# Four wide matmuls without a use are put among the output products of each S5 block

## The chip, the cores and the metric

The kernel runs on one core of a Trainium2 chip. The metric is the device time of one execution in microseconds (us). The engines are called as in the profile: PE is TensorE, with its weight loads shown apart as PEld; DVE is VectorE, ACT is ScalarE, POOL is GpSimd and SP is SyncE. The names with a q (DVEq, SPq, ACTq) are the engines' own sequencers and DMA queues.

## The reference

It is a trunk of two layers over a sequence of 512 tokens of width 1024. Each layer is a half-step SwiGLU feed-forward (FFN), a token mixer, and a second half-step FFN, each behind an RMSNorm with a shift, a scale and a gate from a conditioning vector. The mixer of layer 0 is retention. The mixer of layer 1, which the change touches, is an S5 state space layer:

```python
    bu = jnp.einsum('blgk,gpk->blgp', ug, B_bar)
    a = jnp.broadcast_to(A_bar, (1, L, G, P))
    _, states = lax.associative_scan(combine, (a, bu), axis=1)   # s[t] = A_bar * s[t-1] + bu[t]
    y = jnp.einsum('gkp,blgp->blgk', C_mat, states).real.reshape(Bsz, L, Dm)
    y = jax.nn.gelu(y + d_skip.astype(f32) * uf).astype(u.dtype)
    y1, y2 = jnp.split(y @ w_glu, 2, axis=-1)
    return y1 * jax.nn.sigmoid(y2)
```

There are 64 groups of 16 channels with 64 complex states each.

## The kernel before

All activations are held transposed, with 128 channels on the partitions and the 512 tokens along the free axis, as 8 such tiles. Every large product is made in three parts from a high and a low half of each operand (`mm3`, lines 1309 to 1311). These are single-pass fp32r matmuls with 128x128 weights and 512 moving columns; this text calls them wide. The weights come in chunks of 1024 rows by 256 columns into two buffers, are copied to `w_hi` by ACT and subtracted to `w_lo` by DVE. Chunk n is complete when the semaphore `w_lo_done` stands at n + 2. Chunk 134 (`C_GLU`) is the first one of the S5 layer's GLU and lies in `w_hi[0]`, `w_lo[0]`.

The S5 mixer works on 8 blocks (b) of 8 groups (g). The sequence is cut into 64 pieces of 8 tokens, so that a group's piece is one column of 128 numbers, and a block has 8 x 64 = 512 columns. For each block:

- PE makes the piece inputs of the scan (`states(b)`, line 1505): one plain fp32 matmul for each group, 64 moving columns wide, into bank b % 2 of PSUM. This text calls 64-column fp32 matmuls narrow. The trace shows each of them as two instructions with a weight load each.
- DVE turns them, scans them along the pieces and turns them back into `sc_buf` and `ss_buf` (`scan(b)`), and then signals `sc_done`.
- PE makes the outputs (`outputs(b)`, lines 1518, 1520 and 1521): for each group three narrow matmuls into bank 4 or 6, and then signals `y_done`.
- ACT applies the gelu, writes the block to DRAM and reads it back in token order; ACT and DVE split it into `h_hi` and `h_lo` for the GLU product (`a5_lo` counts them).

PE's order is written out by hand: `states(0)`, and then for each b `states(b + 1)` and `outputs(b)`. The GLU chunks follow behind the last output. SP loads the tables of blocks 6 and 7 behind `y_done` of blocks 2 and 3 in its counting (it waits for counts 3 and 4); they take the place of tables that are used up by then.

Of the kernel before, what the change touches and what calls it, by code (L numbers as in the profile page):

```python
# [13 lines left out]
P = 128  # L14
# [22 lines left out]
C_GLU = 134  # L37
# [53 lines left out]
def build(nc, ins, out):  # L91
    x_d, c_d, pos_d = ins["x"], ins["c"], ins["positions"]
    ctx = ExitStack()
    with ctx:
        def sem(name):
            return ctx.enter_context(nc.semaphore(name))
# [6 lines left out]
        def sb(name, shape, dt=F32, at=None):  # L103
            size = 4 * int(np.prod(shape[1:]))
            if at is None:
                at = place["end"]
                place["end"] = (at + size + 31) // 32 * 32
                assert place["end"] <= nc.sbuf_usable_end, (name, place["end"])
            return nc.alloc_sbuf_tensor_at(name, shape, dt, offset=at)
# [8 lines left out]
        w_hi = [sb(f"w_hi{s}", [P, 8, CW], F32R) for s in range(2)]  # L118
# [82 lines left out]
        ps = ctx.enter_context(nc.psum_tensor("ps", [P, 8, L], F32))  # L201

        w_landed = [sem(f"w_landed{s}") for s in range(2)]
        w_hi_done, w_lo_done, w_used = sem("w_hi_done"), sem("w_lo_done"), sem("w_used")
# [1101 lines left out]
        def _(pe):  # L1306
# [6 lines left out]
            def chunk(n, k, xh, xl, r0, r, bank, first, last, ready=None):  # L1313

                pe.wait_ge(w_lo_done, n + 2)
                s = k % 2
                for t in range(r):
                    if ready is not None:
                        pe.wait_ge(ready[0], ready[1] + t + 1)
                    for c in range(2):  # L1320
                        m = mm3(ps[:, bank + c], w_hi[s][:, t, c * P:(c + 1) * P], w_lo[s][:, t, c * P:(c + 1) * P],
                                xh[:, r0 + t], xl[:, r0 + t], first and t == 0, last and t == r - 1)
                m.then_inc(w_used, 1)
# [173 lines left out]
            def s5():  # L1497
                def states(b):
                    pe.wait_ge(us_in[b], 16)
                    pe.wait_ge(tb_in[b], 16)  # L1500
                    if b >= 2:
                        pe.wait_ge(v_read, b - 1)
                    for g in range(GB):
                        cs = slice(g * NC, (g + 1) * NC)
                        m = nc.tensor.matmul(ps[:, b % 2, cs], tables[b][:, R_WIN + g * P:R_WIN + (g + 1) * P],  # L1505
                                             us[:, b, cs], start=True, stop=True)
                    m.then_inc(v_done, 1)

                def outputs(b):
                    s = b % 2  # L1510
                    pe.wait_ge(sc_done, b + 1)
                    if b >= 2:
                        pe.wait_ge(gelu_done, b - 1)
                    for g in range(GB):
                        cs = slice(g * NC, (g + 1) * NC)
                        o = ps[:, 4 + 2 * s, cs]
                        yw = tables[b][:, R_YS + g * P:R_YS + (g + 1) * P]
                        nc.tensor.matmul(o, tables[b][:, R_MT + g * P:R_MT + (g + 1) * P], us[:, b, cs],  # L1518
                                         start=True, stop=False)
                        nc.tensor.matmul(o, yw, sc_buf[s][:, cs], start=False, stop=False)  # L1520
                        m = nc.tensor.matmul(o, yw, ss_buf[s][:, cs], start=False, stop=True)  # L1521
                    m.then_inc(y_done, 1)

                states(0)
                for b in range(KT):
                    if b + 1 < KT:
                        states(b + 1)
                    outputs(b)
                pe.wait_ge(v_read, KT)
                for dp in range(OUT_PAIRS):  # L1530
                    n = dp * 2 + C_GLU
                    pe.wait_ge(x_done, dp + (5 * OUT_PAIRS + 1))
                    chunk(n, 0, h_hi, h_lo, 0, 8, 0, True, True, ready=None if dp else (a5_lo, 0))
                    chunk(n + 1, 1, h_hi, h_lo, 0, 8, 2, True, True)
# [18 lines left out]
            for q in range(ADA_FIRST):  # L1553
# [3 lines left out]
                for c in range(4):  # L1557
                    m = nc.tensor.matmul(ps[:, 6, c:c + 1], ada_acc[:, c * P:(c + 1) * P], ones[:, 0:1],
                                         start=True, stop=True)
# [10 lines left out]
            ffn(2)  # L1570
            norm(4)
            s5()
            norm(5)
            ffn(3)
# [78 lines left out]
```

## Time and profile before

| what | value |
|---|---|
| median of 3 runs | 2487.16 us (2482.06 to 2487.32) |
| the profiled execution, its own time | 2487.07 us |
| its span, first to last instruction | 2485.3 us |
| mean granted clock of PE over the span | 0.927 |
| PE busy | 2242.6 us, 90% |
| DVE busy | 1167.7 us, 47% |
| ACT busy | 631.3 us, 25% |
| POOL busy | 37.5 us, 2% |

Positions below are microseconds from the start of the span. The granted clock (PEclk) has two levels in this trace: 1.00 is 2.4 GHz and 0.50 is 1.2 GHz. A matmul's duration is longer than the distance to the next one, because they are pipelined. What one costs in a run of them is the distance from start to start, which is read from the timeline or from a stretch and its count.

### The profile page before, as it was taken

The page shows a single profiled execution, that of the slowest core. Times are in us where ns is not written, and L with a number is a line of the kernel's source. Part 1 is how long each engine was busy: PE and PEld are TensorE (multiplying, and loading weights), DVE is VectorE, ACT ScalarE, POOL GpSimd, SP SyncE. Part 2 cuts the span into 40 slices and gives each one's busy share as a digit, 9 for nine tenths or more (in the row PEclk, how much of TensorE's full clock was granted, in tenths as well). Part 3 has the DMA queues.
Part 4 walks back from the last instruction along what each step waited for, and adds up shares of the span by engine and source line. Part 5 has one row for each costly group of instructions (what it writes and reads, how often), then busy time and mean ns, then how long its engine had stood idle before and what let it go on. Part 6 is the DMA issues. An engine that isn't in the chain of part 4 may idle for free.

```text
span 2485.3 us, 26565 instructions
## 1 busy us (share of the span) xinstructions
PE 2242.6 (90%) x10363; PEld 1862.4 (75%) x10363; DVE 1167.7 (47%) x1443; ACT 631.3 (25%) x531; POOL 37.5 (2%) x45
## 2 busy tenths in 40 slices
PE   2499999889999898999998999999949988999996
PEld 1488888778888786888876767678839866888884
DVE  4755544455455325555476655434444334333331
ACT  2222222232223213222221322221220124344221
POOL 1000000000000000000000000000000000000000
PEclk9899999889999998999999889899965698999997
DMA  6245634432232233555454344434683122322220
GB/s 223 68 154 183 203 122 154 163 110 89 68 105 89 84 102 102 173 173 194 130 179 150 129 120 124 117 107 132 219 274 103 50 68 68 101 90 96 93 93 34
DMA packets 264433, 313.07 MB, mean 126 GB/s; under 512 B 31568, under 2 KB 218280, under 8 KB 263096
## 3 DMA queue, kind: packets, MB, share of 16 engines
q1 hardware_dynamic: 224664, 282.66, 34.6%
q10 hardware_dynamic: 39712, 29.63, 4.1%
q8 instruction: 38, 0.62, 0.1%
q14 instruction: 19, 0.16, 0.0%
HBM read 288.93 MB, written 27.53 MB: 127 GB/s over the span
## 4 chain that ended last, share of the span: by engine, by line
PE 50%; issue 34%; DVE 8%; ACT 4%; DMA 2%; ACTq 2%; POOL 1%; SPq 0%; DVEq 0%; POOLq 0%
PE ps L1309 14%; PE ps L1311 14%; PE ps L1310 14%; ACT w_hi L470 1%; DVE ada_acc L756 1%; PE ps L1518 1%; PE ps L1520 1%; PE ps L1521 1%; PE ps L1415 1%; ACTq L607 1%; DVE w_lo L745 1%; PE ps L1505 1%; DVE ys L897 1%; DVE tabs L897 1%; ACT h_hi L470 1%
## 5 line engine op out<-in xcount | busy, mean ns | idle before, releaser
L1309 PE MATMUL ps<-h_hi,w_lo 128*128 128x512 f32 x1792 | 719.7, 402 | 54.5 <-DVE w_lo L745 28.0
L1310 PE MATMUL ps<-h_lo,w_hi 128*128 128x512 f32 x1792 | 711.7, 397 | 0.0
L1311 PE MATMUL ps<-h_hi,w_hi 128*128 128x512 f32 x1792 | 711.3, 397 | 0.0
L745 DVE TENSOR_TENSOR w_lo<-w_raw,w_hi 128x2048 fp32r<-128x2048 f32 (+1 forms) x175 | 392.6, 2243 | 513.6 <-ACT w_hi L470 513.4
L470 ACT ACTIVATE w_hi<-w_raw 128x2048 fp32r<-128x2048 f32 (+1 forms) x176 | 328.9, 1869 | 478.7 <-PE ps L1311 170.0
L1309 PEld LDWEIGHTS ps<-h_hi,w_lo 128*128 128x128 f32 x1792 | 346.5, 193 | 130.0 <-DVE w_lo L745 28.6
L1311 PEld LDWEIGHTS ps<-h_hi,w_hi 128*128 128x128 f32 x1792 | 344.9, 192 | 74.3
L1310 PEld LDWEIGHTS ps<-h_lo,w_hi 128*128 128x128 f32 x1792 | 346.0, 193 | 70.8
L1309 PE MATMUL ps<-g_hi,w_lo 128*128 128x512 f32 x832 | 331.1, 398 | 10.8 <-DVE g_lo L1158 6.9
L1310 PE MATMUL ps<-g_lo,w_hi 128*128 128x512 f32 x832 | 329.9, 396 | 0.0
L1311 PE MATMUL ps<-g_hi,w_hi 128*128 128x512 f32 x832 | 329.8, 396 | 0.0
L756 DVE SCALAR_TENSOR_TENSOR ada_acc<-ada_raw,csil,ada_acc 128x512 f32<-128x512 f32 x224 | 168.5, 752 | 138.2 <-DMA ada_raw<-in_ada_w 126.4
L1309 PEld LDWEIGHTS ps<-g_hi,w_lo 128*128 128x128 f32 x832 | 156.8, 189 | 49.6 <-issue 7.2
L1311 PEld LDWEIGHTS ps<-g_hi,w_hi 128*128 128x128 f32 x832 | 156.7, 188 | 38.5
L1310 PEld LDWEIGHTS ps<-g_lo,w_hi 128*128 128x128 f32 x832 | 156.8, 189 | 37.9
L470 ACT ACTIVATE g_hi<-s_buf 128x1024 f32 (+1 forms) x48 | 51.0, 1062 | 373.0 <-DVE s_buf L873 343.5
L873 DVE TENSOR_TENSOR s_buf<-s_buf,ps 128x1024 f32<-128x1024 f32 x44 | 53.7, 1221 | 156.9 <-PE ps L1311 156.7
L563 ACT ACTIVATE s_buf<-ps 128x1024 f32<-128x1024 f32 x44 | 45.2, 1028 | 211.2 <-PE ps L1311 211.1
L1309 PE MATMUL ps<-w_hi,h_lo 128*128 128x256 f32 x256 | 74.0, 289 | 7.0 <-DVE w_lo L745 7.0
L877 DVE TENSOR_TENSOR g_lo<-s_buf,g_hi 128x1024 f32 (+1 forms) x44 | 53.9, 1225 | 54.5 <-ACT g_hi L470 54.5
L532 ACT ACTIVATE sq<-x_sb 128x1024 f32<-128x1024 f32 (+1 forms) x24 | 25.4, 1059 | 205.1 <-DVE x_sb L825 159.1
L1310 PE MATMUL ps<-w_lo,h_hi 128*128 128x256 f32 x256 | 73.6, 288 | 0.0
(205 smaller groups left out, 1710.0 us busy)
## 6 DMA issues: line engine op xcount, KB each, us to landing
w_raw<-in_ffn_w_in SPq DMA_DIRECT2D x88, 1024.0 KB, 6.7
ada_raw<-in_ada_w SPq DMA_DIRECT2D x128, 512.0 KB, 5.4
w_raw<-in_ffn_w_out SPq DMA_DIRECT2D x32, 1024.0 KB, 7.3
w_raw<-in_ret_w_in SPq DMA_DIRECT2D x24, 1024.0 KB, 5.2
w_raw<-in_ffn_w_out SPq DMA_DIRECT2D x16, 768.0 KB, 4.5
tb<-s_rec SPq DMA_DIRECT2D x6, 2048.0 KB, 10.3
ada_first<-in_ada_w SPq DMA_DIRECT2D x8, 1024.0 KB, 14.3
w_raw<-in_ret_w_out SPq DMA_DIRECT2D x8, 1024.0 KB, 5.0
```

Of the source, the lines that this page charges most:

```text
L470: copy = lambda o, i: nc.scalar.activation(o, i, ACT.Copy)
L532: nc.scalar.activation(sq[:], x_sb[:, tiles, :], ACT.Square).then_inc(sq_done, 1)
L563: nc.scalar.activation(s_buf[:], ps[:, 0:2], ACT.Silu).then_inc(silu_done, 1)
L607: act.dma_start(to[:, :, j * SK:P], lag_out[:, :, 0:P - j * SK]).then_inc(lag_stored, 16)
L745: V.tensor_tensor(w_lo[k % 2][:, 0:r, :], w_raw[k % 2][:, 0:r, :], raw_f32(w_hi[k % 2][:, 0:r, :]), ALU.subtract).then_inc(w_lo_done, 1)
L756: st(V.scalar_tensor_tensor(out=into, in0=raw[:, t], scalar=c, in1=into, op0=ALU.mult, op1=ALU.add))
L873: V.tensor_tensor(s_buf[:], s_buf[:], ps[:, 2:4], ALU.mult).then_inc(prod_done, 1)
L877: V.tensor_tensor(g_lo[:, bass.ds(i * 2, 2), :], s_buf[:], raw_f32(g_hi[:, bass.ds(i * 2, 2), :]), ALU.subtract).then_inc(g_lo_done, 1)
L897: tt = lambda o, a, b, op: st(V.tensor_tensor(o, a, b, op))
L1309: nc.tensor.matmul(o, wl, xh, start=start, stop=False)
L1310: nc.tensor.matmul(o, wh, xl, start=False, stop=False)
L1311: return nc.tensor.matmul(o, wh, xh, start=False, stop=stop)
```

## The change

Behind the three output products of every second group (g = 0, 2, 4, 6), PE issues one more matmul: 128x128 weights from `w_hi[0]`, 512 moving columns from `w_hi[0]` as well, into bank 7, which nothing reads in this stage. That is 4 in each block and 32 in all. Since these read `w_hi[0]`, PE waits once, between `states(0)` and the loop over the blocks, until chunk 134 is complete.

```diff
@@ -1519,9 +1519,12 @@
                                          start=True, stop=False)
                         nc.tensor.matmul(o, yw, sc_buf[s][:, cs], start=False, stop=False)
                         m = nc.tensor.matmul(o, yw, ss_buf[s][:, cs], start=False, stop=True)
+                        if g % 2 == 0:
+                            nc.tensor.matmul(ps[:, 7], w_hi[0][:, 0, 0:P], w_hi[0][:, 0:2, :], start=True, stop=True)
                     m.then_inc(y_done, 1)
 
                 states(0)
+                pe.wait_ge(w_lo_done, C_GLU + 2)
                 for b in range(KT):
                     if b + 1 < KT:
                         states(b + 1)
```

## Rows read from the trace of the kernel before

**Rows 1.** The page: busy tenths and granted clock in 40 slices of 62 us.

```profile
PE   2499999889999898999998999999949988999996
PEclk9899999889999998999999889899965698999997
```

**Rows 2.** Stretch: busy (count) of PE, PEld, DVE, ACT, POOL; clock; DMA share, GB/s.

```profile
1859.24:1961.69 102.45, 102.35 (x480) 102.35 (x481) 46.31 (x62) 7.96 (x13) 7.36 (x7) 0.50 0.24 77
```

**Rows 3.** Timeline (start, us, what): chunk 134's low half, and the first states.

```profile
1808.72 2.29 DVE L745 TENSOR_TENSOR w_lo<-w_raw,w_hi 128x2048 fp32r<-128x2048 f32 x1 [3.40 <-ACT w_hi L470]
...
1841.04 7.09 PE L1505 MATMUL ps<-us,tb 128*128 128x64 f32 x32 [20.74 <-DMA us<-u_dram]
```

**Rows 4.** Waits from 1840 to 1990: us in total, times, longest.

```profile
PE ps L1518 <- DVEq L1230: 11.2, 1, 11.2
...
ACT h_hi L470 <- DMA sq<-y_dram: 4.4, 1, 4.4
```

**Rows 5.** The chain that ended last: the S5 stage's first output and the GLU's first product.

```profile
1859.34 0.69 PE ps L1518 x2
...
1962.00 0.53 PE ps L1309
```

**Rows 6.** Timeline where the narrow matmuls end and the GLU's wide ones begin.

```profile
1961.69 0.33 PEld L1309 LDWEIGHTS ps<-h_hi,w_lo 128*128 128x128 f32 x1
1961.76 0.77 PE L1309 MATMUL ps<-h_hi,w_lo 128*128 128x512 f32 x1
1961.90 0.33 PEld L1310 LDWEIGHTS ps<-h_lo,w_hi 128*128 128x128 f32 x1
...
1962.33 0.63 PE L1310 MATMUL ps<-h_lo,w_hi 128*128 128x512 f32 x1
```

**Rows 7.** Timeline: the first and the last of seven wide matmuls at clock 0.50.

```profile
731.41 0.63 PE L1311 MATMUL ps<-h_hi,w_hi 128*128 128x512 f32 x1
...
733.97 0.63 PE L1311 MATMUL ps<-h_hi,w_hi 128*128 128x512 f32 x1
```

**Rows 8.** Timeline in the third FFN: fp32 transposes between wide matmuls, clock 1.00.

```profile
1425.77 0.39 PE L1311 MATMUL ps<-h_hi,w_hi 128*128 128x512 f32 x1
1426.00 1.03 PE L1403 MATMUL ps<-ident,xs 128*128 128x128 f32 x8
...
1427.11 0.39 PE L1310 MATMUL ps<-h_lo,w_hi 128*128 128x512 f32 x1
```

**Rows 9.** Stretches around two rises of the clock: us, PE busy (x), PEclk, DMA.

```profile
1594.60:1598.00 3.40, 3.40 (x15) 0.50 0.95 307
1598.00:1601.40 3.40, 3.40 (x9) 0.50 0.00 1
1601.50:1604.90 3.40, 3.40 (x16) 1.00 0.00 0
...
1963.30:1966.70 3.40, 3.40 (x10) 0.50 0.27 92
1966.70:1970.10 3.40, 3.40 (x17) 1.00 0.28 63
```

**Rows 10.** Groups of PE's matmuls from 1594.6 to 1598.0 (L1417's left out).

```profile
L1415 PE MATMUL ps<-ys,xs 128*16 128x128 f32 x5 | 1.6, 411 | 0.0
L1309 PE MATMUL ps<-h_hi,w_lo 128*128 128x512 f32 x2 | 1.4, 712 | 0.0
...
L1310 PE MATMUL ps<-h_lo,w_hi 128*128 128x512 f32 x1 | 0.6, 628 | 0.0
L1311 PE MATMUL ps<-h_hi,w_hi 128*128 128x512 f32 x1 | 0.6, 628 | 0.0
```

**Rows 11.** DVE's timeline: first and last step of one S5 block's scan.

```profile
1887.01 1.41 DVE L897 TENSOR_TENSOR tur<-ps,tb 64x512 f32<-64x512 f32 x2 [1.13 <-PE ps L1505]
...
1892.69 0.68 DVE L897 TENSOR_TENSOR sc_buf<-scanned,tb 128x504 f32<-128x504 f32 x1
```

**Rows 12.** DMA issues of the page: KB each, median us to landing.

```profile
tb<-s_rec SPq DMA_DIRECT2D x6, 2048.0 KB, 10.3
```

## The prediction

> **What bounds the kernel now.** I began with the page's two lines in 40 slices [rows 1]. PE is busy nine tenths and more nearly everywhere, so the kernel's time is PE's time, at the clock that PE is granted. The dip of the clock row to 5 and 6 in slices 30 to 32 is the stage of the change: PE is busy 4 tenths in slice 30 and 9 tenths in 31 and 32, at half clock.
>
> Second, the stretch from the first output product to the first GLU product, 1859.24 to 1961.69 [rows 2]: 102.45 us, PE busy for 102.35 of them, clock 0.50 all through. DVE works 46.3 us of it, ACT 8.0, POOL 7.4, and the DMA share is 0.24. It holds 480 narrow instructions: 8 blocks of 48 outputs, and 6 blocks of 16 states (those of blocks 0 and 1 ran ahead, 32 instructions at 1841.04 [rows 3]). 102.4 / 480 = 0.2133 us each.
>
> Third, the waits [rows 4]. PE's last one before the GLU is for DVE's first scan, 11.2 us, and ends at 1859.3; behind it PE waits for nobody. The chain of waits says the same [rows 5]: it leaves DVE at 1859.3 and then stays on PE, narrow matmul after narrow matmul, and goes over to the GLU's wide ones at 1962.0 without a wait between. What is put among the output products is therefore on the path that sets the end, whole, if it takes PE's time.
>
> **The change, part by part.**
>
> *The wait.* It asks for chunk 134's low half. DVE made that at 1808.72, done at 1811.0 [rows 3]. PE comes to the new wait behind the first 16 instructions of 1841.04, some 30 us later. It costs one sequencer step on an engine that afterwards stands idle for 11.2 us waiting for the scan [rows 4]: 0. Behind it stand `states(1)` and all outputs; had the semaphore been late, those would be too, but it has 30 us in hand.
>
> *The 32 wide matmuls.* None is removed, none moved, no DMA is added. All 32 come behind 1859.34. They write bank 7, which no other engine uses here, and read a buffer that is next overwritten after the first GLU chunk. So there is only PE's time to price, and the trace has no such matmul between narrow ones at this clock. I take it from three neighbouring rows.
>
> - At half clock a wide one follows a wide one after (733.97 - 731.41) / 6 = 0.427 us [rows 7].
> - The step from narrow to wide [rows 6]: weight loads start at 1961.69 (wide) and 1961.90, and the second wide matmul at 1962.33. The first wide one's weights took one slot of 0.213, as a narrow one's do, and it then streamed for 0.427. Put between two narrow ones it adds one slot of weights and its streaming time, and hides one narrow load behind its streaming: net 0.427.
> - At full clock both changes of kind are seen [rows 8]. From the wide one at 1425.77 to the first of 8 transposes 0.23 us pass, the plain pace of wide ones. From there to the second wide matmul behind them (1427.11) it is 1.11 us; 8 transposes at 0.110, which is their 1.03 us less the last one's own 0.27 over 7, and one wide one at 0.23 give 1.11. So changing kind costs nothing to speak of.
>
> Sum: 32 x 0.427 = 13.7 us, all on the path, if the clock stays at 0.50.
>
> Bounds. The low one: the engine could run further ahead with weight loads than I read, so that each filler also hides its own load: 0.427 - 0.213 = 0.213, 6.8 us in all. The high one: the recorded starts at the change of kind, 1961.76 against 1962.33, are 0.57 apart, and the chain gives that one 0.53 us [rows 5]; at about 0.54 each it would be 17.3 us. I take 0.427, since it is what the slots on both sides of the change add up to.
>
> *The clock.* This is the term that could be larger than the sum: narrow instructions need about half as long at full clock. In this trace the clock never rises during 102 us of unbroken narrow work [rows 2]. It does rise after the GLU begins: at 1963.30:1966.70 PE ran 10 matmuls, all wide, at 0.50, and the next stretch stands at 1.00 [rows 9]. What a mixture does is seen elsewhere. From 1594.6 to 1598.0, 4 wide ones (4 x 0.427 = 1.7 of 3.4 us) stand with 11 small fp32 ones [rows 9, 10], and the stretch behind it, 9 wide ones, is still at 0.50; only the one after that is at 1.00 [rows 9]. In the changed kernel a filler of 0.43 us stands behind every 12 narrow instructions (2.56 us), and a block's 16 states (3.4 us) have none: 4 x 0.427 = 1.7 us of 15.4 us in a block, 11% wide. That is far thinner than the mixture above, half of it wide, which did not raise it. I take it that the clock stays at 0.50.
>
> The Trainium skill, TensorE: Matmul & The Clock Gate (Part 1, What's actually happening), says that "the default state is throttled, and activity releases the throttle". Taken as meaning busy time, that rule would have S5 at full clock already, since PE has no gap there; the trace has 0.50 at 102.35 of 102.45 us busy, so it does not hold here in that form. Taken as meaning that more columns released it, it is the first rival below; on the forecast's sum it has no bearing.
>
> *What is late next.* Each block takes PE 64 x 0.2133 + 1.7 = 15.4 us in place of 13.65 (the last 13.65 less 3.4 for want of states). DVE's scan takes 6.4 us from 1887.01 to 1893.4 [rows 11] and still ends before its outputs start; the tables need 10.3 us from issue to landing [rows 12] and are asked for two blocks ahead of their use. ACT's last read-back, which it waits for 4.4 us [rows 4], starts with the last output and so moves along with the GLU. No new wait. Nothing behind the stage changes. One thing may shift by chance: how many wide matmuls the GLU runs at half clock before the rise, some 11 before [rows 9], at 0.427 - 0.23 = 0.2 us each: up to 2.2 us either way.
>
> Total: 2487.07 + 13.7 = 2500.7 us against the profiled execution, which lies 0.1 us below the median of the runs, 2487.16. I predict 2500.8.
>
> **The rivals.**
>
> *A. The fillers raise the clock (faster).* The place is the same stretch. At full clock the narrow ones would come every 0.110 us, as the transposes with the same weight load do [rows 8], and the fillers every 0.23: 480 x 0.110 + 32 x 0.23 = 60.2 us in place of 102.4. Blocks would take 64 x 0.110 + 4 x 0.23 = 8.0 us, still longer than the scan's 6.4, and two of them longer than a table's 10.3. The GLU would start at full clock: -2.2. With a first block at half clock (15.4 - 8.0): +7.4. That is 2487.1 - 42.2 - 2.2 + 7.4 = 2450.1. It decides from the point at which full clock holds for a quarter of the stretch: being at full clock all through saves 116.1 - 60.2 = 55.9 us, and 13.7 is a quarter of that (0.245). For it: something wide does raise the clock, always. Against it: the half-wide mixture, and the thin share of 11% [rows 9, 10].
>
> *B. Half of each filler is hidden* (the low bound, weights loaded ahead): 2487.1 + 6.8 = 2493.9. For it speaks that the second wide one's load starts 0.43 us ahead of it (1961.90, 1962.33) [rows 6]; against it the even 0.213 of narrow ones [rows 2].
>
> *C. Each filler costs its change of kind too* (the high bound): 2487.1 + 17.3 = 2504.4. Against it: the transposes among wide ones, which pay nothing for it [rows 8].
>
> *D. It makes no difference.* That needs a wait of PE in the stretch in which the fillers could lie. There is 0.1 us of idle time [rows 2]. It would give 2487.
>
> **How the numbers follow.** Forecast 0.83; A 0.06; B 0.05; C 0.04; D 0.02. The time is the forecast's. Its own spread is the chance shift at the GLU's start and that of the runs shown, 2482 to 2487: 2495 to 2504. The range is 2493 to 2506, which takes in B and C and leaves A and D outside, with under 2 in 10. A measurement of this kernel tells 0.2%, 5 us, from no change. Slower by more than that: forecast, C and nearly all of B, 0.91. Within it: D and a little of B, 0.03. Faster: A, 0.06.
>
> **What the changed profile would show.** The stretch from the first output product to the first GLU product should be 116.1 us long (right: 115 to 117), with 512 instructions of PE and the clock at 0.50 throughout. A filler's neighbours should stand 0.64 us apart (0.213 + 0.427) where they stood 0.213 apart. PE should wait for nothing behind 1859, and the new wait should show no idle time. Wrong in the direction of A: any stretch of S5 at 1.00, and narrow instructions 0.11 us apart. Wrong in B or C: the same clock, and a stretch of 109 or 120 us. The prediction fails if the chip counts narrow fp32 work for more towards the clock than the 102 us at 0.50 let me think, so that one filler in twelve tips it.

## The result, and the profile after

The changed kernel takes 2503.09 us (median of 12 runs, 2496.64 to 2507.17), the kernel before 2488.65 us (12 runs, 2480.27 to 2495.9). The ratio is 1.0053, 95% interval 1.0038 to 1.0068: slower by 13.2 us, with 9.5 to 16.9 for its interval. The prediction had 13.7, and 2500.8 us in a range of 2493 to 2506.

The profiled execution took 2499.44 us, its span is 2497.6. First the stretches of PE between the first output product and the first GLU product, and at the GLU's start, as in [rows 2, 9]. The first row has all engines, the others PE alone, in which PE busy (count), the granted clock and the DMA share follow the length.

```profile
1858.34:1974.44 116.10, 116.00 (x512) 112.93 (x512) 46.35 (x62) 7.96 (x13) 7.38 (x7) 0.50 0.21 68
1975.20:1978.60 3.40, 3.40 (x10) 0.50 0.22 80
1978.60:1982.00 3.40, 3.40 (x17) 1.00 0.33 75
```

The stretch was 102.45 us with 480 instructions and is 116.10 with 512: 13.65 us more, at clock 0.50 from end to end. DVE, ACT and POOL do what they did. The GLU runs at half clock at first, and the clock rises behind some 10 wide matmuls in a row, where it was some 11 before.

The chain of waits, which answers to [rows 5], and PE's waits from 1840 to 1990, to [rows 4]:

```profile
1858.43 0.69 PE ps L1518 x2
1859.12 0.43 PE ps L1520 x2
1859.55 0.43 PE ps L1521 x2
1859.98 0.53 PE ps L1523
...
1974.75 0.53 PE ps L1309
```

```profile
PE ps L1505 <- DMA us<-u_dram: 20.5, 1, 20.5
PE ps L1518 <- DVEq L1230: 11.0, 1, 11.0
```

Line 1523 is the added matmul. It stands on the chain, and PE still has only the two waits that lie ahead of the outputs. The timeline shows one of them with its neighbours; PEld are the weight loads, whose starts are the better clock:

```profile
1859.67 0.33 PEld L1523 LDWEIGHTS ps<-w_hi 128*128 128x128 f32 x1
1859.74 0.77 PE L1523 MATMUL ps<-w_hi 128*128 128x512 f32 x1
1859.88 0.76 PEld L1518 LDWEIGHTS ps<-us,tb 128*128 128x128 f32 x2
...
1860.52 0.55 PEld L1520 LDWEIGHTS ps<-sc_buf,tb 128*128 128x128 f32 x2
```

Between the load at 1859.88 and that at 1860.52 lie two narrow loads, 0.64 us in place of 2 x 0.213: the next load starts later by the 0.427 that the added one streams. That is the 0.213 + 0.427 that the prediction named. The new wait asks for a value that DVE's work of 1807.32 to 1809.61 gave, some 31 us before the first states at 1840.39.

### The profile page after: what moved, and what is told of

The parts are those of the page before. It is cut to its first block, busy times and chain, and to the rows that moved or that the text cites. A ratio compares the mean times of both kernels' runs of the same rounds, so it can differ in the third digit from the quotient of the medians.

```text
span 2497.6 us, 26629 instructions
## 1 busy us (share of the span) xinstructions
PE 2255.0 (90%) x10395; PEld 1871.1 (75%) x10395; DVE 1167.9 (47%) x1443; ACT 631.4 (25%) x531; POOL 37.5 (2%) x45
## 4 chain that ended last, share of the span: by engine, by line
PE 51%; issue 33%; DVE 7%; ACT 4%; ACTq 2%; DMA 1%; POOL 1%; DVEq 0%; SPq 0%; POOLq 0%
PE ps L1309 14%; PE ps L1310 14%; PE ps L1311 14%; ACT w_hi L470 1%; DVE ada_acc L756 1%; PE ps L1415 1%; PE ps L1521 1%; PE ps L1520 1%; ACTq L607 1%; PE ps L1518 1%; PE ps L1505 1%; DVE ys L897 1%; DVE w_lo L745 1%; PE ps L1523 1%; DVE tabs L897 1%
## 5 line engine op out<-in xcount | busy, mean ns | idle before, releaser
L1311 PEld LDWEIGHTS ps<-g_hi,w_hi 128*128 128x128 f32 x832 | 156.4, 188 | 38.4
```

The lines of the kernel that those rows point to most:

```text
L1311: return nc.tensor.matmul(o, wh, xh, start=False, stop=stop)
```

## Experiments

All use one helper and the added wait, unless a diff says otherwise:

```python
                def wide(cols=512):
                    nc.tensor.matmul(ps[:, 7, 0:cols], w_hi[0][:, 0, 0:P], w_hi[0][:, 0:2, :], start=True, stop=True)
```

Each was timed in turns with the kernel before on the same chip; e1 to e4, e5 to e8 with e12, and e9 to e11 ran on three different chips, so ratios compare them better than medians do. "The stretch" is the time from the first output's weight load to the first GLU product's, from the experiment's one profile.

### The price of one: e6, e5, e1

e6 keeps the wait and leaves out the matmuls.

```diff
                 states(0)
+                pe.wait_ge(w_lo_done, C_GLU + 2)
```

> Only the added wait on chunk 134, no added matmul. Theory T: 0 us, within 0.2% of before, the stretch 102.45 us. If the wait had a part in the loss, the start of the second block's states would be later than right behind the first's.

Ratio 0.9998 (0.9982 to 1.0013), and the stretch is as before:

```profile
1855.30:1957.65 102.35, 102.35 (x480) 102.35 (x480) 46.33 (x62) 7.97 (x13) 7.37 (x7) 0.50 0.24 77
```

The wait costs nothing that shows.

e5 has the change's 32 matmuls with 256 moving columns.

```diff
+                        if g % 2 == 0:
+                            wide(256)    # the moving columns are w_hi[0][:, 0, 0:256]
```

> The change with 256 moving columns in each added matmul in place of 512. Theory T says that what one adds is its place in the row of weight loads or its streaming time, whichever is longer: at half clock a load's slot is 0.213 us and 256 columns stream for 0.213 us, so each adds 0.213 us, 6.8 us in all; the stretch from the first output to the first GLU product is 109.3 us at clock 0.50 and the kernel 7 us above before. A rival in which a change between narrow fp32 and fp32r work has a fixed price of its own would show more than 0.213 us each: with 0.32 us, 112.7 us.

Ratio 1.0021 (1.0008 to 1.0034), 5.2 us. The profile is sharper:

```profile
1861.98:1971.16 109.18, 109.18 (x512) 109.18 (x512) 46.34 (x62) 7.96 (x13) 7.37 (x7) 0.50 0.23 73
```

(109.18 - 102.35) / 32 = 0.213 us each, half of what 512 columns cost. The change of kind has no price of its own.

e1 puts one behind every group, 64 in all.

```diff
+                        if True:
+                            wide()
                     m.then_inc(y_done, 1)
```

> The wide matmul stands behind every group (8 in a block, 64 in all) in place of every second. Theory T (each adds 0.427 us to PE's path at half clock and the clock stays down, since a burst of nothing but wide ones is what raises it): the stretch from the first output to the first GLU product is 102.45 + 64 x 0.427 = 129.8 us at clock 0.50, the kernel 27.3 us above before. Rival A (a denser sprinkling raises the clock): some stretch of S5 stands at 1.00 and narrow instructions come every 0.11 us there; the stretch is well under 100 us.

Ratio 1.0092 (1.0075 to 1.0108), 22.9 us by the ratio and 23.1 by the medians (2512.83 against 2489.68).

```profile
1862.10:1991.55 129.45, 129.45 (x544) 123.39 (x544) 46.36 (x62) 7.97 (x13) 7.38 (x7) 0.50 0.19 61
```

The stretch grew by 27.1 us, 0.423 each, as expected, and even twice the density leaves the clock at 0.50. The kernel lost some 4 us less than the stretch, which lies just outside the ratio's interval of 18.7 to 26.9 us. Behind the stage this profile has 521.0 us against 523.6 before, and one fall of the clock fewer in the GLU; yet the two profiled executions, 2514.42 and 2487.07 us, are 27.4 apart. No run takes that apart, and it stays open.

### The same matmuls where PE is idle: e2, e3, e4

If only an unbroken run of wide matmuls raises the clock, that run can be had for nothing: PE stands idle for 11 us ahead of the first outputs [rows 4]. e2 moves all 32 there.

```diff
                     if b + 1 < KT:
                         states(b + 1)
+                    if b == 0:
+                        for _ in range(32):
+                            wide()
                     outputs(b)
```

> The same 32 wide matmuls, but all in a row in PE's idle time between the second block's states and the first block's outputs, none among the outputs. Theory T: the first 11 us of them lie in the wait for DVE's scan and cost nothing; they raise the clock before the outputs begin, and the narrow ones then run every 0.11 us for as long as the clock holds. In the GLU it held 23.9 us after each rise; about 4 of those pass before the outputs, so some 20 us of S5 run at 1.00, which saves about 19 us: the stretch takes 83 us, the kernel about 2469 by the time of before 2488. Rival N (narrow fp32 work pulls the clock down at once, whatever came before): the clock falls back to 0.50 within some 4 us of the first output, stretch about 100 us, kernel within 3 us of before. Rival H (raised once, unbroken narrow work holds it): stretch 480 x 0.11 = 53 to 60 us, kernel 42 to 49 us below before.

Ratio 0.9949 (0.9921 to 0.9977), but its 12 runs are two groups: five at 2462 to 2466 and seven at 2483 to 2494. The profile is of the second group:

```profile
1852.10:1860.90 8.80, 8.80 (x34) 6.87 (x33) 6.28 (x6) 3.20 (x2) 0.00 (x0) 0.84 0.49 160
1860.90:1863.40 2.50, 0.31 (x3) 0.26 (x3) 2.18 (x4) 0.00 (x0) 0.23 (x1) 1.00 0.16 53
1863.40:1865.10 1.70, 1.70 (x18) 1.70 (x17) 1.64 (x3) 0.00 (x0) 0.82 (x1) 1.00 0.00 0
1865.10:1963.40 98.30, 98.30 (x464) 98.30 (x463) 44.54 (x60) 7.96 (x13) 6.31 (x6) 0.50 0.25 81
```

The burst raised the clock, PE then stood idle for 2.2 us, ran 18 narrow instructions at 1.00, and the clock fell. So there is a way to raise it; in this run the gain was gone after 2 us of outputs, and the stretch of some 100 us is that of rival N. The five runs at 2462 to 2466 gain what theory T expected and more, but none of them was profiled.

e3 is e2 with the change's 4 in each block, e4 e2 with 8 in each block.

```diff
+                        if g % 2 == 0:     # e4: if True
+                            wide()
```

> The burst of 32 in PE's idle time, and the change's 4 wide ones in each block as well. It asks if the change's spacing, which can't raise the clock, can hold it once it is up. Theory T by itself does not say; the traces have stretches this thin on both sides. If held throughout: 480 x 0.11 + 32 x 0.23 = 60 us, the kernel some 42 us below before. If it falls after the 23.9 us as without fillers: 83 us + about 11 us for the fillers left at half clock = 92 us, kernel 10 us below before. Rival N: 116 us as in the changed kernel.

> The burst, and 8 wide ones in each block. If this density holds the clock: 480 x 0.11 + 64 x 0.23 = 67.5 us for the stretch, kernel 35 us below before; blocks are then 8.9 us. If it doesn't: some 20 us at 1.00 and the rest at half clock, about 105 us, kernel 2 us above before. Rival N: 130 us, kernel 27 above.

e3: ratio 0.9983 (0.9954 to 1.0012), again two groups, six runs at 2465 to 2478 and six at 2493 to 2507. e4: 1.0094 (1.0079 to 1.0108), one group. The profile of e3 is of its better group:

```profile
1848.90:1858.70 9.80, 9.80 (x34) 7.68 (x33) 7.16 (x8) 3.19 (x2) 0.00 (x0) 0.73 0.49 158
1858.70:1860.20 1.50, 0.38 (x3) 0.20 (x2) 1.25 (x3) 0.00 (x0) 0.18 (x1) 1.00 0.00 0
1860.20:1899.00 38.80, 38.80 (x328) 37.97 (x327) 25.46 (x34) 3.65 (x6) 5.09 (x5) 1.00 0.45 151
...
1899.00:1907.00 8.00, 1.57 (x15) 1.43 (x13) 5.76 (x8) 1.85 (x3) 0.00 (x0) 0.69 0.45 125
1907.00:1947.20 40.20, 39.10 (x172) 37.95 (x172) 15.97 (x21) 2.46 (x4) 2.11 (x2) 0.50 0.10 27
```

328 instructions in 38.80 us at 1.00, against 172 in 40.20 at 0.50. The clock fell in an idle gap of PE. The waits from 1845 to 1990 tell where that comes from, and the DMA issues from 1885 to 1900 why:

```profile
ACT h_hi L470 <- DMA sq<-y_dram: 13.3, 3, 7.5
PE ps L1518 <- DVEq L1230: 8.7, 2, 7.5
```

```profile
tb<-s_rec SPq DMA_DIRECT2D x1, 2048.0 KB, 8.6
sq<-y_dram ACTq DMA_DIRECT2D x1, 256.0 KB, 8.5
```

A read-back of 256 KB takes 8.5 us beside the table loads, where the median before was 2.8. DVE's split of that block stands ahead of its next scan, and PE waits for the scan. In the kernel before, a block's write to DRAM ran beside a table load too (8.0 us, against 2.0 without one), but its read-back came behind that load (2.9 us), and a block of 13.65 us had room for both. In e3 the second table load is issued some 8 us behind the first, before that one has landed (8.6 us), so the write (8.4 us) and the read-back (8.5 us) both run beside one. That they are slow because they share the DMA engines is argued from this coincidence; no run moves the loads. In e4's profile PE stood idle for 2.5 us ahead of the outputs, and the clock fell 1.1 us into them:

```profile
1848.80:1857.10 8.30, 8.30 (x34) 6.62 (x33) 5.82 (x6) 3.19 (x2) 0.00 (x0) 0.88 0.45 146
1857.10:1859.90 2.80, 0.27 (x2) 0.09 (x1) 2.51 (x4) 0.00 (x0) 0.06 (x1) 1.00 0.31 106
1859.90:1861.00 1.10, 1.10 (x10) 1.06 (x10) 1.04 (x2) 0.00 (x0) 1.00 (x1) 1.00 0.00 0
1861.00:1988.00 127.00, 127.00 (x536) 121.04 (x536) 45.32 (x61) 7.97 (x13) 6.33 (x6) 0.50 0.19 62
```

The rest of e4, a stretch of some 128 us and a kernel 23 us above before, is close to rival N. The first row of each burst (with e2's above) also tells when the clock rose: a mean of 0.73 in 9.80 us, 0.84 in 8.80 and 0.88 in 8.30 means 5.3, 2.8 and 2.0 us at half clock, an estimate of 4 to 12 wide matmuls in a row before the rise.

In three profiles the gap ahead of the outputs had 1.1 us of idle time (e3, held), 2.2 (e2, fell) and 2.5 (e4, fell). The next runs close it.

### The gap closed: e7, e8, e10

e7 is e3 with 44 in the burst. e8 adds 24 ahead of the sixth block's outputs, where e3 stood idle. e10 is e7 with one behind every group.

```diff
-                        for _ in range(32):
+                        for _ in range(44):
                             wide()
+                    if b == 5:            # e8 only
+                        for _ in range(24):
+                            wide()
```

> As burst and every second group, with 44 in the burst in place of 32. In the profiles of the three burst runs the burst of 32 ended 1.5, 2.5 and 2.8 us before the outputs began, and the clock fell right afterwards in the last two, and stayed up for 40 us of outputs in the first. Theory I (that idle gap is what decides; closed, the clock stays up in every run through the first blocks): all runs like the better half of e3, 2465 to 2478, none above 2485. Theory R (chance, as where the chip's looks fall, whatever the gap): two groups of runs again, 2470 and 2497.

> e7 with 24 more wide matmuls ahead of the sixth block's outputs, where in e3 PE stood idle for 7.5 us (DVE was held by a read-back that shared the DMA engines with the table loads) and the clock fell. Theory I: the gap is filled, the clock stays up to the end of the stage; stretch about 72 us, kernel 2455 to 2462. If the clock falls elsewhere all the same, it gains nothing on e7 or loses up to 10 us (24 x 0.427).

> The burst of 44 and 8 wide ones in each block. In e4 the clock fell before they could act, behind an idle gap of 2.8 us. Theory I (the gap decided): now it stays up as in e7 until the sixth block, which costs e7's time and 20 x 0.23 + 12 x 0.43 = 9.7 us more: kernel about 2483, against 2512 of e4. If the clock falls all the same: 2512.

e7: ratio 0.9943 (0.9927 to 0.9959), six runs from 2472.65 to 2474.01. The two groups of e3 have become one, as theory I expected: the longer burst, which closes the gap in front of the outputs, took the slower group away. Its clock stayed at 1.00 for 38.4 us of outputs and fell where e3's did, in a gap of 7.4 us ahead of the sixth block's outputs. e8: 0.9935 (0.9918 to 0.9952), 2455 to 2475; in the run that was profiled, the fastest, the second gap was mostly filled too. First the stretch up to 1918 (the whole is 75.6 us), then PE's wait for the scan from 1845 to 1990:

```profile
1856.80:1918.00 61.20, 59.67 (x478) 57.16 (x477) 44.08 (x57) 6.74 (x11) 6.50 (x7) 1.00 0.38 121
```

```profile
PE ps L1518 <- DVEq L1230: 3.2, 2, 1.6
```

Two gaps of 1.5 and 1.6 us were left, ahead of the sixth and the seventh block's outputs; the clock outlasted the first and fell behind the second, at 1921. But most of its runs are at 2470 to 2475, where e7 is, and no profile shows where their clock fell. e10: 0.9901 (0.9867 to 0.9936), five runs at 2448 to 2457 and five at 2480 to 2485. The second group is the expected one, and the profile is of it: the clock fell in a gap of 5.5 us ahead of the sixth block's outputs. The first group was not expected and has no profile. Against e4's 2512 the 12 added matmuls of the burst are worth 27 to 64 us.

### Are those among the outputs of use at full clock? e9, e11, e12

e9 is the burst of 44 and nothing else.

> The burst of 44 with no wide matmul among the outputs. It asks whether the change's 4 in each block are worth anything once the clock is up. Theory K (they hold it): without them the clock falls within a few us of the first outputs, stretch about 100 us, kernel 2485 to 2490 where e7 took 2473. Rival H (narrow work at full clock holds it by itself): the clock stays up until the wait ahead of the sixth block's outputs, the stretch is shorter than e7's by the fillers' 20 x 0.23 + 12 x 0.43 = 9.7 us, kernel about 2464, all runs in one group.

Ratio 0.9901 (0.9886 to 0.9916), 2460 to 2467 in one group, 8 us below e7 by the medians and 10 by the ratios.

```profile
1863.20:1892.00 28.80, 28.38 (x252) 28.25 (x253) 25.58 (x33) 3.05 (x5) 4.21 (x4) 1.00 0.39 125
1892.00:1894.80 2.80, 2.04 (x19) 1.90 (x18) 1.25 (x2) 0.60 (x1) 1.05 (x1) 1.00 0.75 281
1894.80:1942.11 47.31, 45.35 (x214) 45.16 (x214) 21.73 (x28) 4.31 (x7) 2.11 (x2) 0.50 0.24 75
```

Narrow work alone, which never raised the clock, kept it at 1.00 for 28.8 us, and it fell 1.4 us behind the end of the longest gap so far (0.76 us idle in the second row). It was not the first: PE had stood idle for 0.3 us ahead of these rows and for 0.4 us at 1885, and the clock outlasted both. So Theory K falls: narrow work needs no wide matmuls to hold the clock as long as PE has no gap. That they are of no use at full clock does not follow. They lengthen the blocks, and e7, which has them, went 38.4 us without a gap or a fall, where e9's clock fell after 31.6 us and three gaps; and five runs of e10, with twice as many, lie below all six of e9. What they are worth there is open. e11 and e12 put them where gaps are.

```diff
+                    if b in (5, 6, 7):    # e11, with the change's 4 in each block
+                        for _ in range({5: 24, 6: 8, 7: 8}[b]):
+                            wide()
+                    if b >= 4:            # e12, with none among the outputs
+                        for _ in range({4: 8, 5: 20, 6: 8, 7: 8}[b]):
+                            wide()
```

> e8 with 8 more wide matmuls each ahead of the seventh and the eighth block's outputs. In e8's profile PE stood 1.9 us idle ahead of the seventh block's outputs and the clock fell there; its runs spread from 2455 to 2475. Theory I: filled, the clock stays up to the end in most runs, at a price of 16 x 0.23 = 3.7 us less the 1.9 us of idle time: runs at 2450 to 2458. If the spread stays, something else than this gap makes it.

> The burst of 44, then none among the outputs, and bursts of 8, 20, 8 and 8 ahead of the outputs of the fifth to the eighth block. In e9's profile narrow work alone kept the clock at 1.00 for 30 us, and it fell behind PE's first idle gap in it, 1.0 us ahead of the fifth block's outputs. Theory I (wide work is needed only where PE would stand idle): the clock stays up to the end of the stage, stretch 480 x 0.11 + 44 x 0.23 = 63 us, with the gaps filled, kernel about 2450; it is at or below e11's 2460 and e9's 2465. If the fillers among the outputs were of use after all, it falls behind e11.

e11: ratio 0.9883 (0.9866 to 0.9900), 2457 to 2462, somewhat above its expectation of 2450 to 2458. Its clock did not stay up to the end either: it fell at 1909.3, behind a gap of 2.0 us that the burst of 24 ahead of the sixth block's outputs had left, and rose again 17 us later.

```profile
1909.30:1926.30 17.00, 17.00 (x71) 15.94 (x70) 10.45 (x15) 1.23 (x2) 1.05 (x1) 0.50 0.11 32
```

e12: 0.9870 (0.9852 to 0.9888), median 2457.28 against 2490.35, the lowest ratio of all kernels here, though its interval and e11's overlap, and the first group of e10 reaches lower. Its expectation of about 2450 is missed by 7 us, for the clock did fall once more:

```profile
1848.90:1859.80 10.90, 10.90 (x45) 8.87 (x45) 7.96 (x9) 3.20 (x2) 0.00 (x0) 0.91 0.40 131
1860.27:1905.60 45.33, 43.27 (x354) 41.65 (x354) 34.17 (x44) 5.53 (x9) 5.91 (x6) 1.00 0.46 151
1905.60:1922.60 17.00, 17.00 (x74) 16.23 (x73) 11.63 (x15) 1.23 (x2) 1.47 (x2) 0.50 0.11 31
1922.60:1934.57 11.97, 11.97 (x100) 11.62 (x100) 2.78 (x5) 1.23 (x2) 0.00 (x0) 1.00 0.16 45
```

It fell at 1905.6, behind an idle gap of 1.6 us ahead of the sixth block's outputs. It rose again at 1922.6: 8 wide matmuls in a row had stood ahead of the seventh block's outputs, from 1918.07, and the rise came 1 us into the narrow ones behind them. The stretch is 74.3 us, 28 less than before and 6 less than e11's 80.6.

## Why the prediction was right

*The bound.* PE's row of work between the scan and the GLU took every microsecond that was put into it. Shown by the change (13.65 us), e5 (6.83) and e1 (27.1), with PE waiting for nobody.

*The wait at 0.* Shown by e6.

*0.427 us each.* Measured: 13.65 / 32 = 0.427 in the stretch; the low bound (6.8 us in all) and the high one (17.3) are both excluded. e5, with half the columns and half the price, shows what is paid for: the streaming time, while one weight load hides behind it. Fewer than 256 columns were not tried. Rivals B and C are out.

*The clock stays down.* Shown at the change's density and by e1 at twice that. Rival A does not happen in this form. The forecast's own argument for it was weaker than it looks. It rests on the stretch at 1594.6, half of it wide with no rise behind it, but the same trace has a stretch much like it with a rise right behind, 5 wide matmuls with 8 small ones, which the prediction leaves out:

```profile
1475.20:1478.60 3.40, 3.40 (x13) 0.50 0.60 185
1478.60:1482.00 3.40, 3.40 (x16) 1.00 0.60 205
```

In both the small ones come first and the wide ones stand in a row at the end, from 1596.15 and from 1476.38, so neither shows what wide ones scattered among small ones do. The 102 us of narrow work at 0.50 was the sound half of the argument; that 11% of wide work would not tip it was an extrapolation that came true, in part by luck, and was first tested by the changed kernel and e1.

*Nothing behind the stage changes.* The span from the first GLU product to the end is 2485.3 - 1961.69 = 523.6 us before and 2497.6 - 1974.44 = 523.2 after.

*Rival A's price.* This was wrong, though nothing hung on it. It had the stage at full clock limited by PE alone, in 60 us and a kernel of 2450, on the grounds that scan and tables keep up. e3 shows that the read-back beside the table loads does not (8.5 us for 2.8), which costs PE 7.5 us and with them the clock. The best median here, e12's, is 2457; the five unprofiled runs of e10 at 2448 to 2457 come near the 2450, by a way that is not known.

*The rule cited.* The sentence of the Trainium skill (TensorE: Matmul & The Clock Gate, Part 1, What's actually happening) that "activity releases the throttle" agrees with the bursts of wide matmuls, behind which the clock rose in the profiles of e2, e3 and e4. Read as busy time it does not agree: 129.45 us of unbroken mixed work in e1 stayed at 0.50.

Open: of the gaps of 1.5 and 1.6 us in e8 the first left the clock up and the second did not, 1.1 us in e3 left it up and 0.8 in e9 did not, and the runs of e8 and e10 spread over 19 and 37 us. Filling the gaps helped; the length of a gap alone does not decide, and what does was not found.

## What to carry to other kernels

Price a matmul without a use like any other: on a PE-bound path it costs its streaming time, as measured here for 256 and 512 columns at half clock. If it is to raise the clock, it belongs in a row with others, in time in which PE is idle anyway and right up to the work that is to profit; scattered through narrow work at half clock it only makes that work longer (at full clock this is open, see e10). After the clock is up, look for what the faster PE now waits for, since a gap of a microsecond or two can give the rest of it back.

## What the runs showed of the hardware that was not expected

Raising the clock and keeping it are different matters: 64-column fp32 work ran 102 us at 0.50 without raising it [rows 2] and 28.8 us at 1.00 without losing it (e9). The clock then fell behind idle times of PE of 0.8 us (e9), 1.6 us (e8, e12), 2.0 us (e11), 2.2 us (e2) and 2.5 us (e4), and outlasted others of 0.4 us (e9, e12), 1.1 us (e3) and 1.5 us (e8).
